# Dilated attention of a transformer block computed as a near band and four residue classes, merged by maxima and sums

## The chip, the cores and the metric

One NeuronCore of a Trainium2 chip runs the whole program; the other cores do nothing. The metric is the device time of one execution in microseconds, the median of three runs. The hardware profiler recorded one further execution, and every row below comes from it. The engines have the profile's names: PE is TensorE (PEld its weight loads), DVE is VectorE, ACT is ScalarE, POOL is GpSimd, SP is the engine whose queue issues nearly all DMAs.

## The reference

Two transformer layers for 1024 tokens of width 1024. The change lies in the first layer's attention, which has two kinds of heads, eight of each:

```
# dilated heads (depth 64): three patterns (window, dilation), each a softmax of its own
DILATED_PATTERNS = ((128, 1), (512, 4), (2048, 16))
for window, dilation in DILATED_PATTERNS:
    # each query attends to positions i + j*dilation, |j| <= window / (2*dilation)
    o, lse = dilated_window_attention(q, k, v, rel_bias, dilation, window // (2 * dilation))
w = softmax(stack(lses)); out_a = sum(w * outs)      # merged by softmax denominators
# latent heads (nope 64 + rope 32): dense softmax attention over all 1024 keys
out_b = mixer_mla(c_q, c_kv, k_rope, ...)
```

The bias of a dilated head depends only on the distance of key and query (32 buckets). With dilation 1 a query reaches keys at most 64 positions away; with dilations 4 and 16 it reaches only keys in its own residue class modulo 4. The rest of the layer (output projection, routed experts) and the second layer come after and are not touched.

## The kernel before, in words

The program is a row of stages, each with its own buffers, with a barrier between them. `front` projects the tokens and leaves q, k and v of all heads in DRAM, and for each dilated head a skewed table of bias plus the logarithm of the number of patterns that hold the distance (-1e30 where none does). So the three patterns become one dense masked softmax. Stage `att` then runs `attend_heads` over 16 heads, first the eight dilated ones, then the eight latent ones.

A head is cut into 8 units of 128 queries against all 1024 keys. Every engine has a program of its own, a loop over steps n, and works at unit n minus some lag:

- PE: `score(n)`, `turn_p(n-2)` (transposes of the probabilities), `weigh_half(n-4)` (probabilities times values, for two units at once, 256 columns wide), and for every second unit `turn_back`.
- DVE: the row maxima of unit n (for a dilated head one pass, L385, that also adds the table), then for unit n-2 the low halves `pT_lo` (L396) of the probabilities: float32 operands are split into a high and a low part for the matmuls.
- ACT: the high halves `pT_hi` (L343) of unit n-2, then the exponentials of unit n with their row sums.
- POOL: splits the next head's q, k and v into high and low parts.
- SP: for head j the loads of q, k, table and v, then the store of head j-2, in program order, each behind its semaphore waits.

Scores, probabilities and biased scores each have two buffers; the transposed probabilities in PSUM (`pT_ps`) and the weighed sum (`oT_ps`) have one. Engines work strictly in the order of their programs, and so does SP's queue.

## Time and profile before

| | us |
|---|---|
| median of 3 runs (4217.86 to 4221.16) | 4218.14 |
| the profiled execution | 4229.26 |
| its span | 4227.5 |
| attention stage, first to last row maximum | 275.6 to 679.9 |
| PE busy over the span | 3820.9 (90%) |
| DVE, ACT, POOL busy over the span | 2119.5, 1981.5, 1233.9 |

The span is the time from the first to the last instruction of the profiled execution; that execution took 1.8 us more than its span. The attention stage is about a tenth of the program. Busy time of PE counts matmuls whose ends overlap, so that a busy PE is not a PE at its peak.

### The profile page before, as it was taken

The numbers are of one execution on the slowest core, as the hardware profiler recorded it, in microseconds if no ns is written. First come the engines' busy times: TensorE is split into PE (matmuls) and PEld (weight loads), VectorE is DVE, ScalarE is ACT, GpSimd is POOL, SyncE is SP. The second block draws the span as 40 slices with busy tenths as digits, with TensorE's granted clock in tenths as the row PEclk, the third lists the DMA queues.
The fourth block names the chain that finished last, engine by engine and source line by source line (L and its number), as shares of the span: only waits on it lengthen the run. The fifth ranks groups of instructions, "written<-read, shape, count | busy, mean of one in ns | idle before, by whom it ended". The sixth has DMA issues, their size and how long they took to land. (4 is left out here: it accounts for less than half of the span.)

```text
span 4227.5 us, 55120 instructions
## 1 busy us (share of the span) xinstructions
PE 3820.9 (90%) x20567; PEld 3209.4 (76%) x20567; DVE 2119.5 (50%) x3777; ACT 1981.5 (47%) x3487; POOL 1233.9 (29%) x732
## 2 busy tenths in 40 slices
PE   8989997969986999999488875797999999999998
PEld 6879996847755777887388875797888768888886
DVE  3348875267754333320566757674234237533453
ACT  5248766337756545522366654564324234323331
POOL 0024430000004322311133244121631103876541
PEclk9999998969998999999699997998999999999999
DMA  3744223479957222222322212113653112222542
GB/s 118 251 134 118 51 51 105 184 273 420 421 241 255 90 80 80 89 94 74 90 61 79 80 55 79 46 46 115 227 161 117 68 50 90 87 88 85 188 148 98
DMA packets 336536, 548.38 MB, mean 130 GB/s; under 512 B 116451, under 2 KB 209507, under 8 KB 325219
## 3 DMA queue, kind: packets, MB, share of 16 engines
q1 hardware_dynamic: 318348, 478.76, 34.1%
q10 hardware_dynamic: 10720, 39.85, 2.4%
q0 software_dynamic: 7200, 26.22, 1.6%
q8 instruction: 166, 2.72, 0.3%
q14 instruction: 102, 0.84, 0.1%
HBM read 400.63 MB, written 144.11 MB: 129 GB/s over the span
## 5 line engine op out<-in xcount | busy, mean ns | idle before, releaser
L2739 POOL TENSOR_TENSOR mid_w_lo<-mid_w_raw,mid_w_hi 128x1024 fp32r<-128x1024 f32 (+1 forms) x64 | 153.0, 2395 | 406.2 <-ACT mid_w_hi L2927 406.2
L3473 POOL TENSOR_TENSOR end_w_lo<-end_w_raw,end_w_hi 128x1024 fp32r<-128x1024 f32 x60 | 147.2, 2460 | 334.4 <-ACT end_w_hi L3815 334.3
L3097 PE MATMUL mid_ps<-mid_w_hi,mid_xT_hi 128*128 128x512 f32 x576 | 229.0, 398 | 2.7 <-DVE mid_xT_lo L2801 2.7
L3097 PE MATMUL mid_ps<-mid_w_lo,mid_xT_hi 128*128 128x512 f32 x576 | 224.7, 390 | 0.0
L3097 PE MATMUL mid_ps<-mid_w_hi,mid_xT_lo 128*128 128x512 f32 x576 | 224.7, 390 | 0.0
L4131 PE MATMUL end_ps<-end_w_hi,end_xT_hi 128*128 128x512 f32 x544 | 214.7, 395 | 0.0
L4131 PE MATMUL end_ps<-end_w_hi,end_xT_lo 128*128 128x512 f32 x544 | 212.3, 390 | 0.0
L4131 PE MATMUL end_ps<-end_w_lo,end_xT_hi 128*128 128x512 f32 x544 | 211.9, 390 | 0.0
L957 DVE SCALAR_TENSOR_TENSOR moe_w_lo<-moe_wgu,moe_gcol,moe_w_hi 128x512 fp32r<-128x512 f32 x272 | 185.5, 746 | 7.7 <-ACT moe_w_hi L1097 7.7
L343 ACT ACTIVATE att_pT_hi<-att_pT_ps 128x512 fp32r<-128x512 f32 x256 | 139.1, 596 | 99.7 <-PE att_pT_ps L36 99.6
L1097 ACT ACTIVATE moe_w_hi<-moe_wgu,moe_gcol 128x512 fp32r<-128x512 f32 x272 | 173.2, 715 | 2.5 <-DMA moe_wgu<-in_w_gate_up 2.5
L3477 POOL TENSOR_TENSOR end_w_lo<-end_w_raw,end_w_hi 128x1024 fp32r<-128x1024 f32 x60 | 149.0, 2488 | 68.4 <-ACT end_w_hi L3829 68.4
L918 POOL DMA_INDIRECT moe_xb<-xrows,moe_idx x34 | 32.3, 951 | 467.1 <-PE moe_x_ps L36 272.9
L396 DVE TENSOR_TENSOR att_pT_lo<-att_pT_ps,att_pT_hi 128x512 fp32r<-128x512 f32 x256 | 163.6, 681 | 1.9 <-ACT att_pT_hi L343 1.9
L3097 PE MATMUL mid_ps<-mid_xT_hi,mid_w_hi 128*128 128x512 f32 (+1 forms) x400 | 155.9, 390 | 0.0
L3097 PE MATMUL mid_ps<-mid_xT_lo,mid_w_hi 128*128 128x512 f32 (+1 forms) x400 | 155.9, 390 | 0.0
L3097 PE MATMUL mid_ps<-mid_xT_hi,mid_w_lo 128*128 128x512 f32 (+1 forms) x400 | 155.9, 390 | 0.0
L2828 DVE SCALAR_TENSOR_TENSOR mid_conv<-mid_raw,mid_taps,mid_conv 128x1024 f32<-128x1024 f32 x96 | 145.6, 1517 | 3.4
L3503 POOL TENSOR_TENSOR end_w_lo<-end_w_raw,end_w_hi 128x1024 fp32r<-128x1024 f32 x44 | 110.2, 2511 | 122.4 <-ACT end_w_hi L3867 122.4
L4168 PE MATMUL end_ps<-end_w_hi,end_xT_hi 128*128 128x512 f32 x352 | 137.8, 391 | 2.9 <-issue 2.9
L286 PE MATMUL att_oT_ps<-att_pT_hi,att_v_both 128*128 128x256 f32 x512 | 137.8, 303 | 0.5 <-ACT att_oT L334 0.5
L4168 PE MATMUL end_ps<-end_w_hi,end_xT_lo 128*128 128x512 f32 x352 | 137.6, 391 | 0.0
(641 smaller groups left out, 11565.8 us busy)
## 6 DMA issues: line engine op xcount, KB each, us to landing
moe_wgu<-in_w_gate_up SPq DMA_DIRECT2D x34, 2048.0 KB, 11.6
moe_wd<-in_w_down SPq DMA_DIRECT2D x34, 1024.0 KB, 14.1
mid_w_raw<-in_w_in SPq DMA_DIRECT2D x60, 512.0 KB, 4.0
end_w_raw<-in_w_ffn_out SPq DMA_DIRECT2D x44, 512.0 KB, 3.7
end_w_raw<-in_w_ffn_in SPq DMA_DIRECT2D x40, 512.0 KB, 4.3
expert_rows<-moe_out ACTq DMA_DIRECT2D x34, 512.0 KB, 11.3
in_tail<-mid_y SPq DMA_DIRECT2D x56, 256.0 KB, 2.1
qkvT<-mid_conv SPq DMA_DIRECT2D x24, 512.0 KB, 4.4
```

What stands on the lines that cost most here:

```text
L286: ins = pe.matmul(oT_ps[:, 0:2 * P], v, part[:, m % 2, c], start=(c == 0 and k == 0), stop=(c == NT - 1 and k == len(parts) - 1))
L343: act.activation(pT_hi[:, m % 2, at, u * P:(u + 1) * P], pT_ps[:, at], ACT.Copy).then_inc(hi_p, 1)
L396: dve.tensor_tensor(pT_lo[:, m % 2, at, u * P:(u + 1) * P], pT_ps[:, at], pT_hi[:, m % 2, at, u * P:(u + 1) * P].bitcast(F32), ALU.subtrac ...
L957: dve.scalar_tensor_tensor(out=w_lo[:, n % 2, k], in0=wgu[:, n % GR, k], scalar=gcol[:, k:k + 1], in1=w_hi[:, n % 2, k].bitcast(F32), op0= ...
L1097: act.activation(w_hi[:, n % 2, k], wgu[:, n % GR, k], ACT.Copy, scale=gcol[:, k:k + 1]).then_inc(w_hi_set, 1)
L2739: pool.tensor_tensor(w_lo[:, c % 2, 2 * q:2 * q + 2, 0:wid], w_raw[:, 2 * q:2 * q + 2, 0:wid], w_hi[:, c % 2, 2 * q:2 * q + 2, 0:wid].bitc ...
L2828: ins = dve.scalar_tensor_tensor(out=conv[:, j], in0=src, scalar=w, in1=conv[:, j], op0=ALU.mult, op1=ALU.add)
L3097: ins = pe.matmul(o_, lhsT, rhs, start=(k == 0 and part == 0), stop=(k == KC - 1 and part == 2))
L3473: pool.tensor_tensor(halves(w_lo, piece), w_raw[:, 2 * q:2 * q + 2], halves(w_hi, piece).bitcast(F32), ALU.subtract).then_inc(w_split, 1)
L3477: pool.tensor_tensor(slot_of(w_lo, s), factor[s % 7], slot_of(w_hi, s).bitcast(F32), ALU.subtract).then_inc(w_split, 1)
L4131: ins = pe.matmul(o_, lhsT, rhs, start=(k == 0 and part == 0), stop=(k == KC - 1 and part == 2))
L4168: ins = pe.matmul(ps[:, 2 * t + j], xx[:, i % 8, t * P:(t + 1) * P], down_slot(ww, i)[:, j], start=(k == 0 and part == 0), stop=(k == KB - ...
```

## The change

`front` now takes the tokens in residue order (all tokens that are 0 modulo 4, then 1, 2, 3), so q, k and v of all heads lie in that order in DRAM, and the outputs are stored back in natural order. The bias row of a head shrinks from 2048 to 1184 numbers.

A new function `attend_both` replaces `attend_heads` for the first layer (the second layer still calls `attend_heads`). Its heads alternate: dilated, latent, dilated, latent. A latent head is computed as before, in 8 units. A dilated ("sparse") head has 4 units. Unit t holds four segments of 128 queries by 256 keys: two of the near band (32 positions of each of the four residue classes as queries, 64 of each class as keys) and two of the far part (128 queries of class t against the 256 keys of the class). Each segment has its own maximum, exponential and sum. The weighed sum of a segment is no longer transposed: the probabilities are the stationary operand, the values (high and low half side by side, 128 columns) the moving one, and DVE adds the two halves (`tensor_reduce` into `keep`). The near results are in another query order than the far ones, so SP writes them to a DRAM tensor `near` (four DMAs) and reads them back (one); then DVE takes the higher maximum (`highest`), ACT the weights, DVE the shares, and POOL makes the merged output.

```
+            @block.sync
+                def load_table(j):
...
+                    first, second, far = jobs[j]["bias"]
+                    for w in range(2):
+                        sp.dma_start(view[:, w + 1, 0], first).then_inc(table_in[i % 2], 16)
+                        sp.dma_start(view[:, w, 1], second).then_inc(table_in[i % 2], 16)
+                    sp.dma_start(view[:, 0, 0, :, EDGE:], first[:, :, EDGE:]).then_inc(table_in[i % 2], 16)
+                    sp.dma_start(view[:, 2, 1, :, 0:EDGE], second[:, :, 0:EDGE]).then_inc(table_in[i % 2], 16)
+                    for c in range(STRIDE):
+                        sp.dma_start(table[c * BLOCK:(c + 1) * BLOCK, i % 2, 3 * SEG:], far[c]).then_inc(table_in[i % 2], 16)
...
+                def move_near(j):
+                    i = rank[j]
+                    sp.wait_ge(kept, sparse_by[last_unit[j]])
+                    for c in range(STRIDE):
+                        dst = jobs[j]["near"][c * CLASS:(c + 1) * CLASS].rearrange("(t u) d -> u t d", u=BLOCK)
+                        sp.dma_start(dst, keep[c * BLOCK:(c + 1) * BLOCK, i % 2, 0]).then_inc(near_out, 16)
+                    sp.wait_ge(near_out, 16 * STRIDE * (i + 1))
+                    sp.dma_start(keep[:, i % 2, 2], jobs[j]["near"].rearrange("(t p) d -> p t d", p=P)).then_inc(near_in, 16)
...
+                for i in range(H // 2 + 1):
+                    if i < H // 2:
+                        load(2 * i)
+                        load(2 * i + 1)
+                    if i:
+                        move_near(2 * i - 2)
+                        store(2 * i - 2)
+                        store(2 * i - 1)
...
+                def weigh_sparse(n):
...
+                    outcome_taken(n)
+                    pe.wait_ge(lo_p, 2 * n + 2)
+                    for g in range(SEGS):
+                        i = 2 * t + g % 2
+                        for b in range(2):
+                            v = near_both[:, rank[j] % 2, i + b] if g < 2 else v_both[:, j % 2, 2 * t + b]
+                            for k, part in enumerate((pT_hi, pT_lo)):
+                                ins = pe.matmul(oT_ps[:, g * P:(g + 1) * P], split_at(part, n)[:, 2 * g + b], v,
+                                                start=(b == 0 and k == 0), stop=(b == 1 and k == 1))
...
+                def tops_sparse(n):
...
+                    for g in range(SEGS):
...
+                        ch.add(dve.tensor_tensor_reduce(biased[:, n % 2, here], s_ps[:, n % 2, here], table[:, i, at:at + SEG],
+                                                        1.0, -3e38, ALU.add, ALU.max, keep[:, i, g // 2, w, DV:DV + 1]))
+                    ch.wait()
...
+                def highest(j):
+                    both = keep[:, rank[j] % 2, 1:3]
+                    dve.wait_ge(near_in, 16 * (rank[j] + 1))
...
+                for n in range(U + 6):
+                    for j in range(0, H, 2):
+                        if n == last_unit[j] + 7:
+                            highest(j)
+                    if n >= 5 and n - 5 < U and is_sparse[n - 5]:
...
+                        dve.tensor_reduce(keep[:, rank[j] % 2, 0:2, 2 * t:2 * t + 2, 0:DV], found, AX.X, ALU.add).then_inc(kept, 1)
...
+                        if not sparse[j] and n == last_unit[j] + 6:
...
+                            dve.tensor_tensor(o[:, j % 2], o_ps[:], inverse[:, i % 2].unsqueeze(2).to_broadcast([P, NT, DV]), ALU.mult).then_inc(o_out, 1)
...
+                def merge(j):
+                    i = rank[j]
+                    pool.wait_ge(share_set, i + 1)
...
+                for j in range(H):
+                    if j:
+                        split_queries(j)
+                    if sparse[j]:
+                        order_queries(j)
+                    if j:
+                        split_keys(j)
+                    split_values(j)
...
+                    if sparse[j] and j:
+                        merge(j - 2)
...
-    attend_heads(nc, "att", ident, dilated + latent)
+    attend_both(nc, "att", ident, dilated, latent)
```

**SP's queue, around one dilated head.** Before, in the middle of the dilated heads: the store of a head (L223, which waits for that head's `o_out`), then the loads two heads ahead (names are the tiles, "<-" their source).

```order
L223 DMA mixed<-att_o 128x8x64 [waits att_o_out]
L197 DMA att_qT<-qkT_a 64x1024 [waits att_split_q]
L199 DMA att_qT<-qkT_a 64x1024
L206 DMA att_kT<-qkT_a 64x1024 [waits att_split_k]
L208 DMA att_kT<-qkT_a 64x1024
L213 DMA att_table<-skew 128x1920 [waits att_topped]
L219 DMA att_v<-v_a 128x8x64 [waits att_split_v]
```

After, the end of one turn of SP's loop: ahead of these rows stand the four stores of the latent head before (L630, waits `att_o_out`), four loads of q and k and ten of the table.

```order
L591 DMA att_v<-v_a 128x8x64 [waits att_split_v]
L596 DMA att_v_near<-v_a 16x64
L597 DMA att_v_near<-v_a 32x8x64
L602 DMA att_v_near<-v_a 32x9x64 x2
L599 DMA att_v_near<-v_a 32x8x64
L600 DMA att_v_near<-v_a 16x64
L557 DMA att_qT<-qkT_b 96x1024 [waits att_split_q]
L565 DMA att_kT<-qkT_b 96x1024 [waits att_split_k]
L591 DMA att_v<-v_b 128x8x64 [waits att_split_v]
L619 DMA near<-att_keep 32x8x66 [waits att_kept]
L619 DMA near<-att_keep 32x8x66 x3
L621 DMA att_keep<-near 128x8x66 [waits att_near_out]
```

The copy of the near results out and back (L619, L621) stands in the queue behind four stores and all loads for the next two heads, 28 DMAs in all.

**DVE, the row maxima of one unit of a dilated head.** Before: one pass over 1024 columns with its read of the maximum, then the low halves of unit n-2.

```order
L383 MEMSET att_pad 128x1 [waits att_exped,att_scored]
L385 ISA att_biased,att_top<-att_s,att_table 128x1024
L385 ISA att_top 128x1
L389 TENSOR_SCALAR att_neg_top<-att_top 128x1 [waits att_dve_steps]
L396 TENSOR_TENSOR att_pT_lo<-att_pT_ps,att_pT_hi 128x4x128 [waits att_hi_p] x2
```

After: four passes over 256 columns, each with its read.

```order
L819 MEMSET att_pad 128x1 [waits att_exped,att_scored]
L827 ISA att_biased,att_keep<-att_s,att_table 128x256
L827 ISA att_keep 128x1
L827 ISA att_biased,att_keep<-att_s,att_table 128x256
L827 ISA att_keep 128x1
L827 ISA att_biased,att_keep<-att_s,att_table 128x256
L827 ISA att_keep 128x1
L827 ISA att_biased,att_keep<-att_s,att_table 128x256
L827 ISA att_keep 128x1
L830 TENSOR_SCALAR att_neg_top<-att_keep 128x4 [waits att_dve_steps]
L871 TENSOR_TENSOR att_pT_lo<-att_pT_ps,att_pT_hi 128x512 [waits att_hi_p] x2
```

The unit has the same 1024 columns of scores but there are half as many units; the passes are four.

**DVE, inside the latent head that follows a dilated one.** After, the end of its fifth step, all of its sixth, and its seventh up to the first low halves; before, such a step has only a maximum, its scaling and two low halves.

```order
L871 TENSOR_TENSOR att_pT_lo<-att_pT_ps,att_pT_hi 128x4x128 [waits att_hi_p] x2
L859 TENSOR_REDUCE att_top<-att_s 128x1 [waits att_exped,att_scored]
L860 TENSOR_SCALAR att_neg_top<-att_top 128x1 [waits att_dve_steps]
L871 TENSOR_TENSOR att_pT_lo<-att_pT_ps,att_pT_hi 128x4x128 [waits att_hi_p] x2
L836 TENSOR_TENSOR att_higher<-att_keep 128x8 [waits att_near_in]
L837 TENSOR_TENSOR att_gap<-att_keep,att_higher 128x16 [waits att_dve_steps]
L859 TENSOR_REDUCE att_top<-att_s 128x1 [waits att_exped,att_scored]
L860 TENSOR_SCALAR att_neg_top<-att_top 128x1 [waits att_dve_steps]
L871 TENSOR_TENSOR att_pT_lo<-att_pT_ps,att_pT_hi 128x4x128 [waits att_hi_p] x2
```

The wait for the near results (`att_near_in`) stands ahead of the seventh step's row maximum and low halves.

## Rows read from the trace of the kernel before

**Rows 1.** The score tile's readers: ns min/median/max, first and last start

```profile
L385 DVE CUSTOM_DVE_ANT_0 att_biased<-att_s,att_table x64: 1219/1220/1225, 275.6 to 459.6; 128x1024 f32<-128x1024 f32 x64
L388 DVE TENSOR_REDUCE att_top<-att_s x64: 1211/1225/1226, 462.8 to 679.9; 128x1 f32<-128x1024 f32 x64
```

**Rows 2.** Windows: us; busy PE, PEld, DVE, ACT, POOL; PEclk, DMA share, GB/s

```profile
300.00:460.00 160.00, 160.00 (x1184) 147.97 (x1183) 143.34 (x339) 129.47 (x242) 69.63 (x39) 1.00 0.36 92
470.00:680.00 210.00, 210.00 (x1466) 190.90 (x1465) 162.41 (x261) 143.89 (x274) 68.05 (x39) 1.00 0.19 41
```

**Rows 3.** Timeline of TensorE over one latent unit: start us, us, instruction

```profile
560.85 0.55 PE L302 MATMUL att_o_ps<-att_fold,att_oT 128*128 128x64 f32 x4
561.21 0.47 PE L261 MATMUL att_s<-att_k_hi,att_q_hi 96*128 96x512 f32 x1
...
562.67 1.04 PE L36 MATMUL att_pT_ps<-att_ident,att_p 128*128 128x128 f32 x8
563.47 0.37 PE L286 MATMUL att_oT_ps<-att_pT_hi,att_v_both 128*128 128x256 f32 x1
...
564.50 0.40 PE L261 MATMUL att_s<-att_k_hi,att_q_hi 96*128 96x512 f32 x1
```

**Rows 4.** Timeline of VectorE over one dilated unit

```profile
370.27 1.22 DVE L385 CUSTOM_DVE_ANT_0 att_biased<-att_s,att_table 128x1024 f32<-128x1024 f32 x1 [0.59 <-issue]
...
371.42 0.08 DVE L385 DVE_READ_ACCUMULATOR2_ANT att_top<- 128x1 f32 x1
371.54 0.15 DVE L389 TENSOR_SCALAR att_neg_top<-att_top 128x1 f32<-128x1 f32 x1
371.61 1.28 DVE L396 TENSOR_TENSOR att_pT_lo<-att_pT_ps,att_pT_hi 128x512 fp32r<-128x512 f32 x2
```

**Rows 5.** A 256-wide tile of the last stage, the same view as rows 1

```profile
L3612 DVE TENSOR_REDUCE end_soft<-end_ps x32: 414/424/426, 3366.9 to 3431.5; 128x1 f32<-128x256 f32 x32
...
L3941 ACT ACTIVATE end_scratch<-end_ps,end_soft x32: 468/473/478, 3367.5 to 3436.3; 128x256 f32<-128x256 f32 x32
```

**Rows 6.** 128-column matmuls of the delta stage, timeline and tile view

```profile
2145.54 1.05 PE L1940 MATMUL delta_ps<-delta_inv,delta_Z 128*128 128x128 f32 x8
...
L1940 PE MATMUL delta_ps<-delta_inv,delta_Z x512: 272/276/582, 2094.9 to 2554.7; 128*128 128x128 f32 x171
```

**Rows 7.** Timeline of SP's queue, attention stage and delta stage

```profile
386.06 0.59 SPq L197 DMA_DIRECT2D att_qT<-qkT_a  x1
386.69 0.60 SPq L199 DMA_DIRECT2D att_qT<-qkT_a  x1
...
2049.02 3.77 SPq L1427 DMA_DIRECT2D delta_lower<-delta_L  x8
2054.04 0.49 SPq L1432 DMA_DIRECT2D delta_small<-delta_lower  x1
```

**Rows 8.** DMA issues of three stretches: xcount, KB each, median us to landing

```profile
mixed<-att_o SPq DMA_DIRECT2D x7, 256.0 KB, 2.7
...
att_qT<-qkT_a SPq DMA_DIRECT2D x16, 256.0 KB, 4.4
...
att_v<-v_b SPq DMA_DIRECT2D x6, 256.0 KB, 5.7
...
delta_lower<-delta_L SPq DMA_DIRECT2D x64, 16.0 KB, 1.7
```

**Rows 9.** Query splitting on POOL in the attention stage, tile view

```profile
L418 POOL TENSOR_TENSOR att_q_hi<-att_qT,att_one x9: 1890/1893/1905, 277.5 to 462.0; 128x1024 fp32r<-128x1024 f32 x7, 96x1024 fp32r<-96x1024 f32 x2
L421 POOL TENSOR_TENSOR att_q_hi<-att_qT,att_q_hi x7: 2388/2395/2414, 279.5 to 416.9; 64x1024 fp32r<-64x1024 f32 x7
```

**Rows 10.** Timeline of POOL at the start of the attention stage

```profile
266.71 0.10 POOL L445 MEMSET att_one<- 128x1 f32 x1 [265.82 <-issue]
```

**Rows 11.** Windows around an idle stretch of TensorE, columns as in rows 2

```profile
1230.00:1236.20 6.20, 0.34 (x4) 0.11 (x1) 1.47 (x3) 2.43 (x5) 0.00 (x0) 0.85 0.21 85
1236.20:1241.20 5.00, 4.90 (x16) 4.26 (x17) 5.00 (x8) 5.00 (x8) 0.00 (x0) 0.50 0.00 0
```

More of the change, by code:

```diff
@@ L21 @@
 SLOTS = 4
+STRIDE = 4
+NEAR, AFAR = 96, 512
+BIAS = (2 * STRIDE - 1) * NEAR + AFAR
+NEVER = -1e30
 @contextmanager
@@ new lines, in bias_constants, with reach @@
+def bias_constants(T, buckets, max_distance, patterns):
+    block, edge = P // STRIDE, P // STRIDE // 2
+    steps = np.arange(NEAR)[None] - (block + edge - 1)
+    near = (STRIDE * steps + np.arange(1 - STRIDE, STRIDE)[:, None]).reshape(-1)
+    far = STRIDE * (np.arange(AFAR) - (T // STRIDE - 1))
+    def reach(rel, pairs):
+        n = np.abs(rel)
+        return sum(((n % d == 0) & (n // d <= w // (2 * d)) & (n < T)).astype(np.float64) for w, d in pairs)
+    assert all(d == 1 or d % STRIDE == 0 for w, d in patterns)
+    rel = np.concatenate([near, far])
+    count = np.concatenate([reach(near, [(w, d) for w, d in patterns if d == 1]), reach(far, [(w, d) for w, d in patterns if d > 1])])
@@ L2523, in _ @@
                 pe.wait_ge(hot_in, 32)
-                for b in range(4):
-                    pe.matmul(ps[0:A_HEADS, 4 + b], values[:], onehot[:, b * BANK:(b + 1) * BANK], start=True, stop=True).then_inc(hot_done, 1)
+                for b in range(BIAS_BANKS):
+                    wid = min(BANK, BIAS - b * BANK)
+                    pe.matmul(ps[0:A_HEADS, 4 + b, 0:wid], values[:], onehot[:, b * BANK:b * BANK + wid], start=True, stop=True).then_inc(hot_done, 1)
                 pe.wait_ge(const_in, 16)
@@ L4210, in table @@
-    def table(h):
-        return skew[h:h + 1, P - 1:P - 1 + P * W - P].rearrange("h (p w) -> (h p) w", w=W - 1)[:, 0:W - P]
-    dilated = [dict(depth=A_DIM, dv=A_DIM, q=qkT_a[h * A_DIM:(h + 1) * A_DIM], k=qkT_a[AW + h * A_DIM:AW + (h + 1) * A_DIM],
-                    v=tiles(v_a[:, h * A_DIM:(h + 1) * A_DIM]), out=tiles(mixed[:, h * A_DIM:(h + 1) * A_DIM]),
-                    scale=A_DIM ** -0.5, bias=table(h)) for h in range(A_HEADS)]
-    latent = [dict(depth=NOPE + ROPE, dv=B_DIM, q=qkT_b[h], k=qkT_b[B_HEADS + h],
-                   v=tiles(v_b[:, h * B_DIM:(h + 1) * B_DIM]),
-                   out=tiles(mixed[:, AW + h * B_DIM:AW + (h + 1) * B_DIM]), scale=(NOPE + ROPE) ** -0.5, bias=None) for h in range(B_HEADS)]
@@ L4219, in build_program, with tables, block, far @@
-    attend_heads(nc, "att", ident, dilated + latent)
+    mixed, near = dram("mixed", (T, AW + B_HEADS * B_DIM)), dram("near", (A_HEADS, T, A_DIM + 2))
+    def tables(h):
+        rows, width, pitch = P // STRIDE, BIAS - 1, STRIDE * NEAR
+        def block(ahead):
+            at = (STRIDE - 1) * NEAR + rows - 1 + ahead
+            flat = skew[h, at:at + P * width].rearrange("(p w) -> p w", w=width)
+            return flat[:, 0:pitch].rearrange("p (c z) -> p c z", z=NEAR)[:, :, 0:rows]
+        def far(c):
+            at = c * (rows * width + NEAR - rows) + (2 * STRIDE - 1) * NEAR + P - 1
+            return skew[h, at:at + rows * width].rearrange("(p w) -> p w", w=width)[:, 0:3 * P]
+        return block(0), block(rows), [far(c) for c in range(STRIDE)]
@@ new lines, in by_class_out @@
+    def by_class_out(columns):
+        return mixed[:, columns].rearrange("(h p c) d -> c p h d", c=STRIDE, p=P)
+    dilated = [dict(depth=A_DIM, dv=A_DIM, q=qkT_a[h * A_DIM:(h + 1) * A_DIM], k=qkT_a[AW + h * A_DIM:AW + (h + 1) * A_DIM],
+                    v=v_a[:, h * A_DIM:(h + 1) * A_DIM], out=by_class_out(slice(h * A_DIM, (h + 1) * A_DIM)),
+                    scale=A_DIM ** -0.5, bias=tables(h), near=near[h]) for h in range(A_HEADS)]
+    latent = [dict(depth=NOPE + ROPE, dv=B_DIM, q=qkT_b[h], k=qkT_b[B_HEADS + h], v=v_b[:, h * B_DIM:(h + 1) * B_DIM],
+                   out=by_class_out(slice(AW + h * B_DIM, AW + (h + 1) * B_DIM)), scale=(NOPE + ROPE) ** -0.5, bias=None) for h in range(B_HEADS)]
```

456 lines of the change are left out of this document (435 added, 21 removed).

## The prediction

> **What bounds the kernel now.** Only the attention stage changes much, so I read that stage alone. First the view of the score tile gives its pace: the row maxima of the 64 dilated units start from 275.6 to 459.6 us, those of the 64 latent units from 462.8 to 679.9 [rows 1]. Divided by 63 that is 2.92 us per dilated unit and 3.45 per latent unit; 64 of each make 407.7 us. Then the windows show which engine fills it: PE is busy all of 160.00 and 210.00 us at full clock; DVE is busy 143.34 and 162.41 of it, ACT 129.47 and 143.89 [rows 2]. PE sets the pace of both kinds. In a latent unit DVE works 162.41/210 x 3.45 = 2.67 us, so it has 0.8 to spare; the dilated part has all engines close together.
>
> The timeline splits PE's latent unit [rows 3]: scores from 561.21 to 562.67 (1.46 us), transposes to 563.47 (0.80), weighing to 564.50 (1.03), and every second unit 0.36 of turning back (560.85 to 561.21): 3.47 with half of the last, as measured.
>
> **A sparse unit.** Eight score matmuls of 256 columns: the eight weighing matmuls of 256 columns took 1.03 [rows 3], so 1.0. Transposes 0.80 as before. In the four steps of a sparse head PE still weighs latent units (1.03 + 0.18), because weighing lags by four steps; so these steps cost PE 3.0.
>
> DVE: before, the pass over 1024 columns took 1.15 until its read, 0.12 to the scaling, 0.07 to the low halves, 1.28 for both [rows 4]. A reduction over 256 columns takes 0.424 where one over 1024 takes 1.225 [rows 1, 5], so a pass over 256 saves 0.80: 0.35 until its read, and 0.11 for the read. Four are 1.85 and the step is 1.85 + 0.07 + 1.28 + some 0.15 of waits = 3.35. The low bound is PE's 3.0; the high one 4.1, if no pass starts before the last has fully ended (4 x (0.42 + 0.12 + 0.12) = 2.65 in place of 1.85). I take 3.35, since the trace shows DVE's ends overlapped. ACT was busy 129.47/160 x 2.92 = 2.36 per unit; four exponentials at 0.473 [rows 5] in place of one of 1024 columns (1.22, if ACT's takes as long as DVE's) add 0.7, so 3.1, below DVE.
>
> **The latent steps behind it.** In the first four latent steps PE weighs sparse units: 16 matmuls of 128 columns. The delta stage issues eight such in 1.05 us, of which 0.276 is the last one's own time [rows 6]: 0.110 apart, so 16 take 1.78 with 0.1 to begin. The step is 3.45 - 1.03 - 0.18 + 1.88 = 4.12. DVE's new sum of halves is a 512-wide pass like one low half, 0.64 [rows 4]; with 2.67 it is 3.3 and lies under PE.
>
> The Trainium skill ("TensorE: Matmul & The Clock Gate", section "Back-to-back issue gap") gives 81 ns for a sustained 128-column matmul with its weight load. By that 16 would be 0.5 us cheaper and the 32 such steps 16 us, and the kernel would come to about 4211 us. The row shows 0.110, in a run of eight like the sixteen here, and the sum goes by the row; the rule gets no chance of its own.
>
> A pair (4 sparse, 8 latent units) is then 4 x 3.35 + 4 x 4.12 + 4 x 3.45 = 43.7. The merge's small operations on DVE add some 0.5 where its slack is used up. POOL adds 0.3: after the shares it merges (estimate 1.9 + 1.3) and splits the next latent head's q and k, 1.9 + 2.4 each [rows 9], 11.8 in all, while the sparse head lasts 13.4 and the score must be there 1.6 earlier. So 44.5 a pair, 356 for eight, **51.7 us less** than 407.7.
>
> **Start and end.** POOL starts its program at 266.71 [rows 10] and now clears pads first, on which the first table load waits; the first score also waits for the reordered queries, one POOL pass of 1.9 [rows 9]: 2 us. Before the first latent head POOL splits two sets of values (passes of 512 and 576 columns, about half of those of 1024, 4.6 us after they land) and then q and k (8.6) [rows 9]: 13.2 against a sparse block of 13.4, with the landing of some 4 us ahead of it: 4 us. Three more stores at the end, 0.47 each: 1.3. Together **7.3 us more**. The front's shorter bias moves fewer bytes with more DMAs under a PE that is busy: nothing; uncovered it would be 24 DMAs of 0.47, 11 us.
>
> **The wait that I expect.** Let latent head B follow sparse head A. DVE waits for A's near results at B's seventh step, ahead of that step's maximum and low halves; behind it wait ACT's exponential, PE's transposes and so everything. The near copy stands in SP's queue behind 28 DMAs, and the first of these, a store of the latent head before A, waits for an output that DVE makes at the end of B's second step. From there:
> - Issue: 4 stores and 17 table and value loads at 3.77/8 = 0.47, six q and k loads at 386.69 - 386.06 = 0.63, one more value load: 14.1 us [rows 7].
> - Near out: 1.4 to the start of the fourth issue; the landing of such a write 1.7 [rows 8]. In the delta stage SP in fact waits for eight small writes, from 2049.02 + 3.77 to 2054.04, before it reads them back [rows 7].
> - Near in: 1024 pieces of 264 bytes; a store of the same size and 256-byte pieces lands in 2.7 [rows 8]; I take 3.0. Sum 20.3.
> - Queue: a value load right behind a latent head's q and k takes 5.7 [rows 8], 2.7 more. Between 0 and 2.7 I take 2.7, since the copy stands just there. Sum 23.0.
>
> DVE needs it after steps three to six, 2 x 4.12 + 2 x 3.45 = 15.1, and 0.8 of slack: 15.9. It is **7.1 us late** (bounds 0, if the issues overlap more than in rows 7, and 14, if each of the 28 takes the longest spacing, 0.63, and the queue counts for the way out and the way in). PE falls idle, and after an idle stretch the trace shows it at half clock: 6.2 us idle, then 5.0 at a granted clock of 0.50 [rows 11], the lower of the two levels (1.2 GHz). That costs up to 2.5, here 1.7. So 8.8 a pair, in six pairs of eight: the first pair's copy and the last one's have no loads ahead of them that wait. **53 us more.**
>
> Sum: -51.7 + 7.3 + 53 = +9. The profiled execution of 4229.3 would take 4238. The median of the runs lies 11 us lower; I add the same 9 to 4218: **4227 us**.
>
> **Rivals.**
> - *The copy is in time.* If the 28 issues and the round trip take under 16 us, nothing waits and 51.7 - 7.3 = 44 us are won: 4174. For it: the eight writes of the delta stage were issued at 0.47 and had all landed 1.25 us after the last issue [rows 7], without a backlog. Against it: even without a queue the sum is 20.3. It decides at 15.9 us from the latent output. With halfway cases, 0.25.
> - *The sparse unit is DVE's.* At the high bound of 4.1, 0.75 x 4 x 8 = 24 us more: 4251. For it: four short passes and four reads that depend on one semaphore. Against it: DVE's passes overlap in rows 4. 0.15.
> - *Small pieces choke the DMA queue.* Table, near values and near results now move in pieces of 64 to 264 bytes, before the table moved in 7680. If each 256 KB of these took 1 us longer, some 5 us a pair would fall on the copy, 30 us in six pairs: 4257. Against it: 256 KB in 256-byte pieces lands in 2.7 us, in pieces of 4 KB in 4.4 [rows 8]. The Trainium skill ("DMA: Bandwidth & Descriptors", section "Specifications") asks for at least 512 bytes a transfer for line rate; rows 8 show no such loss. 0.15.
> - *No change that can be told.* A measurement of this kernel can tell about 0.2%, 8.4 us. My forecast lies just outside this band and half of its cases inside it.
>
> **How the numbers follow.** The forecast (copy late by 4 to 9 us, 4210 to 4250) has 0.45. Faster: the first rival's 0.25 and 0.05 of the forecast, 0.30. Within 0.2%: 0.22, nearly all of it the forecast's. Slower: the rest of the forecast 0.18, and the two slow rivals 0.30: 0.48. The range reaches from the copy in time to the far end of the slow rivals, 4178 to 4275; beyond lie the page's cheap matmuls on top of the first rival, and two slow rivals at once.
>
> **What would show it.** Right: sparse steps of 3.3 us with DVE full, four latent steps of 4.1 with PE full; DVE idle 5 to 8 us ahead of `att_higher` (L836) once a pair from the second on, released by a DMA from `near`, and PE at 0.5 behind it; SP issuing without a pause for some 14 us ahead of L619. Wrong: no such idle time, then the time falls by 40 us; or sparse steps near 4 us; or the landing of `near` far longer than 3 us.

## The result and the profile after the change

| | before | after |
|---|---|---|
| median of 4 runs, us | 4219.65 (4217.86 to 4223.98) | 4261.58 (4258.21 to 4266.70) |
| the profiled execution | 4229.26 | 4266.70 |
| its span | 4227.5 | 4264.6 |
| first to last instruction of the attention stage | 429.2 | 467.9 |

The kernel before has one run more here than above. The ratio is 1.0099 (95% interval 1.0081 to 1.0116): the change costs 42 us in the medians and 37 in the profiled executions. The forecast was 4227, +9, in a range of 4178 to 4275: the direction and the range hold, the size does not.

The stage tells where. The tile view of `near`, the DRAM copy of the near results (SP's two lines that move it, and who waits for it):

```profile
L619 SPq DMA_DIRECT2D near<-att_keep x32: 303/472/1576, 310.8 to 702.1; - x32
L621 SPq DMA_DIRECT2D att_keep<-near x8: 376/377/380, 314.9 to 704.3; - x8
...
  DVE att_higher L836: 73.6, 7
DMA to landing us min/median/max: 1.8/4.7/5.7
```

VectorE is idle for 73.6 us in seven waits for the copy: 1.0 in the first pair of heads, 72.6 in the next six, 12.1 each (11.5 to 12.7). The eighth does not wait. VectorE's timeline at the second pair:

```profile
360.56 0.15 DVE L860 TENSOR_SCALAR att_neg_top<-att_top 128x1 f32<-128x1 f32 x1
360.63 1.28 DVE L871 TENSOR_TENSOR att_pT_lo<-att_pT_ps,att_pT_hi 128x512 fp32r<-128x512 f32 x2
374.25 0.17 DVE L836 TENSOR_TENSOR att_higher<-att_keep 128x8 f32<-128x8 f32 x1 [12.34 <-DMA att_keep<-near]
374.46 0.18 DVE L837 TENSOR_TENSOR att_gap<-att_keep,att_higher 128x16 f32<-128x16 f32 x1
374.56 1.21 DVE L859 TENSOR_REDUCE att_top<-att_s 128x1 f32<-128x1024 f32 x1
```

TensorE stops with it. In the windows around that wait and over two whole pairs (columns as in [rows 2]) it is idle from 366.2 to 376.7, works at the granted clock 0.50, the lower level (1.2 GHz), up to about 382, and a pair lasts 58 us of which it is busy for 46:

```profile
366.00:376.00 10.00, 0.16 (x1) 0.00 (x0) 1.68 (x5) 0.01 (x1) 3.63 (x3) 0.64 0.50 93
376.00:379.00 3.00, 2.30 (x11) 2.33 (x12) 2.96 (x5) 2.22 (x5) 0.00 (x0) 0.50 0.00 0
379.00:382.00 3.00, 3.00 (x16) 3.00 (x15) 1.47 (x6) 1.75 (x4) 1.19 (x1) 0.50 0.00 0
...
383.60:441.68 58.08, 46.12 (x322) 42.16 (x322) 39.29 (x93) 31.22 (x78) 29.19 (x18) 0.88 0.36 74
441.68:499.48 57.80, 46.11 (x321) 42.13 (x320) 39.33 (x92) 31.08 (x78) 29.19 (x18) 0.88 0.37 74
```

Why the copy is late stands in SP's timeline of the same pair. `o_out`, the semaphore on which the store of the latent head before waits, was set at 347.33, and SP issued without a pause from there to the copy:

```profile
328.40 20.86 SPq L630 DMA_DIRECT2D mixed<-att_o  x8
349.30 0.48 SPq L557 DMA_DIRECT2D att_qT<-qkT_a  x1
...
354.02 1.75 SPq L580 DMA_DIRECT2D att_table<-skew  x1
...
356.36 2.29 SPq L583 DMA_DIRECT2D att_table<-skew  x4
...
363.17 0.43 SPq L591 DMA_DIRECT2D att_v<-v_b  x1
363.64 3.08 SPq L619 DMA_DIRECT2D near<-att_keep  x4
371.33 0.38 SPq L621 DMA_DIRECT2D att_keep<-near  x1
```

(The first row holds eight stores, the last four of them from 347.35 to 349.26.) The near sums had been complete at 355.32; their copy was issued 8.3 us later because of its place in the queue (experiment 1 shows that nothing else held it).

The other lines answer to [rows 3] and [rows 4] and show the work itself as it was worked out. One of the latent steps that weigh a sparse unit, on TensorE: 16 weighing matmuls of 128 columns (first two and last), then the next score.

```profile
351.82 1.04 PE L40 MATMUL att_pT_ps<-att_ident,att_p 128*128 128x128 f32 x8
352.61 0.30 PE L710 MATMUL att_oT_ps<-att_near_both,att_pT_hi 128*128 128x128 f32 x1
352.75 0.28 PE L710 MATMUL att_oT_ps<-att_near_both,att_pT_lo 128*128 128x128 f32 x1
...
354.32 0.28 PE L710 MATMUL att_oT_ps<-att_v_both,att_pT_lo 128*128 128x128 f32 x1
354.43 0.45 PE L676 MATMUL att_s<-att_k_hi,att_q_hi 96*128 96x512 f32 x1
```

They take 354.43 - 352.61 = 1.82 us, 0.112 apart behind the first; 1.88 was forecast, and the step lasts 4.06 in place of 4.12. The 81 ns of the Trainium skill ("TensorE: Matmul & The Clock Gate", section "Back-to-back issue gap") do not appear here either.

One line has no counterpart in the forecast: VectorE's scaling of four maxima (L830, 128x4). Its view, and one of its long ones behind the passes of its step (the first two and the last read), with POOL's instruction that ran beside it:

```profile
L830 DVE TENSOR_SCALAR att_neg_top<-att_keep x32: 169/524/1741, 274.2 to 682.6; 128x4 f32<-128x4 f32 x32
...
389.89 0.41 DVE L827 CUSTOM_DVE_ANT_0 att_biased<-att_s,att_table 128x256 f32<-128x256 f32 x1
390.24 0.08 DVE L827 DVE_READ_ACCUMULATOR2_ANT att_keep<- 128x1 f32 x1
390.24 0.41 DVE L827 CUSTOM_DVE_ANT_0 att_biased<-att_s,att_table 128x256 f32<-128x256 f32 x1
...
390.93 0.08 DVE L827 DVE_READ_ACCUMULATOR2_ANT att_keep<- 128x1 f32 x1
391.04 1.73 DVE L830 TENSOR_SCALAR att_neg_top<-att_keep 128x4 f32<-128x4 f32 x1
392.68 1.27 DVE L871 TENSOR_TENSOR att_pT_lo<-att_pT_ps,att_pT_hi 128x512 fp32r<-128x512 f32 x2
...
390.33 2.40 POOL L919 TENSOR_TENSOR att_k_lo<-att_kT,att_k_hi 96x1024 fp32r<-96x1024 f32 x1
```

It lasts 0.17 us where POOL is idle and 1.73 here; it ends at 392.77, POOL's instruction at 392.73. Below such an instruction is called held. 22 of the 32 scalings are long, and each ends 0.02 to 0.03 us behind a POOL instruction. In the kernel before none of the 128 scalings (128x1) lasts over 0.16.

### The profile page after: what moved, and what is told of

Same layout as the page of the kernel before. It is cut to its first block and busy times, and to the rows that moved or that the text cites. A ratio compares the mean times of both kernels' runs of the same rounds, so it can differ in the third digit from the quotient of the medians.

```text
span 4264.6 us, 54593 instructions
## 1 busy us (share of the span) xinstructions
PE 3773.8 (88%) x20181; PEld 3166.8 (74%) x20181; DVE 2087.5 (49%) x3841; ACT 1925.4 (45%) x3526; POOL 1296.6 (30%) x782
## 5 line engine op out<-in xcount | busy, mean ns | idle before, releaser
L4666 PE MATMUL end_ps<-end_w_hi,end_xT_lo 128*128 128x512 f32 x544 | 212.0, 390 | 0.0
L4666 PE MATMUL end_ps<-end_w_lo,end_xT_hi 128*128 128x512 f32 x544 | 211.7, 389 | 0.0
L40 PE MATMUL att_pT_ps<-att_ident,att_p 128*128 128x128 f32 x768 | 111.5, 289 | 69.5 <-DVE att_pT_lo L871 64.4
L40 PEld LDWEIGHTS att_pT_ps<-att_ident,att_p 128*128 128x128 f32 x768 | 94.7, 149 | 86.3 <-issue 67.8
L784 ACT ACTIVATE att_pT_hi<-att_pT_ps 128x512 fp32r<-128x512 f32 x192 | 104.5, 592 | 106.5 <-PE att_pT_ps L40 106.5
L4703 PE MATMUL end_ps<-end_w_lo,end_xT_hi 128*128 128x512 f32 x352 | 138.0, 392 | 0.0
```

The source lines that it names most:

```text
L40: return pe.transpose(out, tile, ident[:])
L4666: ins = pe.matmul(o_, lhsT, rhs, start=(k == 0 and part == 0), stop=(k == KC - 1 and part == 2))
L4703: ins = pe.matmul(ps[:, 2 * t + j], xx[:, i % 8, t * P:(t + 1) * P], down_slot(ww, i)[:, j], start=(k == 0 and part == 0), stop=(k == KB - ...
```

## Experiments

Each number of the kernel before stands beside runs on the same chip; the ratio of the changed kernel, to compare with, is 1.0099. "A pair" is the time from the first maxima of one sparse head to those of the next, read from VectorE's timeline; "a sparse step" goes from the start of one scaling of the maxima to the next, so that the first begins in the last latent step. Profiles are compared by the length of the attention stage, since the stages behind it, with the same code in all 14, differ by up to 12 us among them.

**1. The latent head's store later in SP's order**

```diff
+                    if i >= 2:
+                        store(2 * i - 3)
                     if i:
                         move_near(2 * i - 2)
                         store(2 * i - 2)
-                        store(2 * i - 1)
+                store(H - 1)
```

Expected: 

> The edit moves only the latent head's four stores in SP's order: behind the loads for the next two heads and ahead of the near copy one turn later, so the loads no longer stand behind a store that waits for `o_out`. Theory A (the near copy is late because of its place in SP's queue): in six pairs the wait at `att_higher` falls from 12.1 us (11.5 to 12.7) to under 1.5, a pair lasts about 45 us as the undisturbed last one does (44.9) in place of 57.8, and the kernel gains 6 x 12.9 = 77 us: 4262 - 77 = 4185, range 4175 to 4200. Theory B (the loads' own traffic holds the copy, wherever it stands): the copy still takes over 10 us from the last kept sum to its landing and the wait stays at 5 us or more: over 4215. Theory C (the wait hides another one, such as POOL's splitting of the next head): the wait goes, but a pair stays above 50 us: over 4215 too, with the idle time at another instruction.

Measured: 4187.05 us beside 4225.61, ratio 0.9913 (0.9897 to 0.9930). The view of the waiting line, L838 in this kernel:

```profile
L838 DVE TENSOR_TENSOR att_higher<-att_keep x8: 173/173/175, 318.1 to 628.3; 128x8 f32<-128x8 f32 x8
...
  DMA att_keep<-near: 3.6, 6
```

The wait fell from 73.6 us to 3.6, and a pair lasts 44.5 us: six in a row lie between 44.50 and 44.55. The first write is issued 0.03 us after the last kept sum, and from the second pair on the results are back 6.7 to 7.3 us after it. Theory A holds; this change of order alone was worth 1.0099 - 0.9913 = 0.0186, 79 us.

**2. The near copy on ScalarE's queue**

```diff
+                        if n == last_unit[j] + 5:
+                            near_away(j)
+                        if n == last_unit[j] + 6:
+                            near_back(j)
```

`near_away` waits for the kept sums and issues the four writes, `near_back` waits for them and issues the read.

Expected: 

> The near copy, out and back, is issued by ScalarE's queue instead of SP's; SP keeps its order for the rest. Theory A (place in SP's queue): the four writes leave within 3 us of the last kept sum, the results land back some 7 us after it, the wait at `att_higher` falls from 12.1 to 0 to 3 us, and 60 to 75 us are won, less at most 8 for ScalarE's five issues a pair at 0.5: 4190 to 4210. Theory B (the traffic of SP's loads on the DMA engines holds the copy): the writes go out at once but take 5 us to land and the read more than 3; the wait stays at 5 or more: over 4220.

Measured: 4234.11 us, ratio 1.0022 (1.0011 to 1.0032). The tile view of `near`:

```profile
L753 ACTq DMA_DIRECT2D near<-att_keep x32: 309/482/724, 315.5 to 669.4; - x32
L758 ACTq DMA_DIRECT2D att_keep<-near x8: 382/383/442, 319.5 to 671.9; - x8
...
  DVE att_higher L844: 46.4, 8
  ACT att_p L808: 7.4, 4
DMA to landing us min/median/max: 1.8/3.1/7.8
```

The writes left 1.6 us after the last kept sum, as theory A has it, but the results came back late all the same: waits of 4.8 to 8.0 us in the six pairs. At the second pair the read took 7.8 us to land (2.9 in the changed kernel), while SP issued its loads beside it, from the table at 355.32 to the latent values at 366.87. In the first and the last pair, where no loads were under way, the read on the same queue took 3.0. By its time and its waits this is theory B: a queue of its own ends the wait to be issued, 5.0 of the 12.1 us, and not the delay beside the loads. The core's DMA engines were busy for 0.98 of the time while the second pair's read was under way, 0.45 and 0.41 in the first and the last pair; that the loads' packets kept it waiting there is likely, not tested by itself. The first experiment ends both, since it moves the loads ahead: there, from the second pair on, the last write lands in 2.2 to 2.6 us and the read in 2.9 to 3.4.

**3. The table in longer pieces** (one execution)

```diff
-                        sp.dma_start(view[:, w + 1, 0], first).then_inc(table_in[i % 2], 16)
+                        sp.dma_start(table[:, i % 2, (w + 1) * SEG:(w + 1) * SEG + P], wide[:, 0:P]).then_inc(table_in[i % 2], 16)
```

and so for all six near loads of the table, which then holds other numbers than the biases. Expected: 

> The six near loads of a head's table fetch rows of 128 neighbouring numbers, pieces of 512 bytes (768 of them) in place of 3072 pieces of 128 and 64; the count of DMAs stays, the values are not the table's. Theory A (the 28 issues and the queue behind the latent head's q, k and v make the copy late): the wait at `att_higher` falls by 2 us at most, the stall of 1.2 us in issuing the fifth table load: 4250 to 4262. Theory B (small pieces choke the queue): the wait falls by 5 us or more, 30 us in six pairs: under 4235.

Measured: 4254.02 us. The waits are 64.8 us in seven, 10.6 in each of the six pairs in place of 12.1; the first write goes out 15.0 us after `o_out` in place of 16.7, mostly since the fifth table load (1.75 us above) now takes 0.43, and the writes still take 5.4 to land. Theory A: the table's small pieces cost 1.5 us of the 12. The fifth load:

```profile
357.01 0.43 SPq L579 DMA_DIRECT2D att_table<-skew  x1
```

**4. Ten issues fewer** (one execution)

```diff
-                    if sparse[j]:
+                    if sparse[j] and rank[j] < 2:
                         load_table(j)
...
```

The later heads use the tables of the first two, and VectorE waits for these alone. Expected: 

> The table loads of the third to eighth sparse head are left out (these heads use the tables of the first two, so the values are wrong); everything else is as in the changed kernel. Of the 28 issues ahead of the near copy 10 go. Theory A (the issues' number is the larger part of the lateness): the first write of the copy is issued 5.5 to 6.5 us earlier after `o_out` (16.7 before), lands as late as before (5 us, behind the latent head's q, k and v), and the wait at `att_higher` falls from 12.1 to 5.5 to 7: 30 to 40 us in six pairs, 4225 to 4237. Theory B (the table's small pieces choke the queue): the landing of the writes falls from 5 us to 2.5 too, and the wait to 4 or less: under 4220.

Measured: 4237.66 us. The first write goes out 10.7 us after `o_out`, 6.0 earlier; the writes still take 5.7 to land; the waits are 6.2 to 6.9 us in the six pairs, 6.5 on average. Theory A, 0.7 us beyond its far end in time: ten issues of 28 are 5.6 of the 12.1 us.

**5. Four scalings of one column**

```diff
-                    dve.tensor_scalar(neg_top[:, n % 4].rearrange("p (k s) -> p k s", k=2), keep[:, i, 0:2, 2 * t:2 * t + 2, DV],
-                                      -jobs[j]["scale"], None, ALU.mult).then_inc(topped, 1)
+                    for g in range(SEGS):
+                        w = 2 * t + g % 2
+                        ins = dve.tensor_scalar(neg_top[:, n % 4, g:g + 1], keep[:, i, g // 2, w, DV:DV + 1],
+                                                -jobs[j]["scale"], None, ALU.mult)
+                    ins.then_inc(topped, 1)
```

Expected: 

> The edit replaces VectorE's one scaling of four maxima (128x4) by four scalings of one column (128x1); the order of all queues stays. In the changed kernel the 128x4 scaling lasts 0.17 us when POOL is idle and up to 1.74 when POOL is in a tensor_tensor, and 22 of 32 end 0.02 to 0.03 us after the POOL instruction that ran. Theory A (VectorE is held by the running POOL instruction, which a one-column scaling is not, as in the latent units, where none is held): the 3.1 us a pair of held time go, the sparse steps of 3.5, 3.95 and 4.3 us come to 3.0 to 3.3, minus some 0.2 for three more scalings: 2 to 2.5 us a pair, 16 to 20 in all, 4242 to 4246. Theory B (the long records are only drawn to the next instruction, and something else sets the step): no change within 5 us, 4262, and the four scalings' rows show the same time in another place.

Measured: 4250.79 us, ratio 1.0064 (1.0048 to 1.0081): by the ratios 15 us under the changed kernel, by the medians and by the stage (456.7 us) 11, less than the 16 to 20 expected. The view of the line, which answers to that of L830:

```profile
L832 DVE TENSOR_SCALAR att_neg_top<-att_keep x128: 142/145/155, 273.4 to 672.5; 128x1 f32<-128x1 f32 x128
```

No scaling is held, though POOL runs beside them as before, and the third sparse step lasts 2.95 us in place of 3.9 to 4.1 (five of the pairs). That VectorE was held is theory A; a pair won 1.0 us by it (six pairs), not 2 to 2.5, and the first pair 3.3.

**6. Later store and four scalings**

Expected: 

> The later store of the first experiment (0.9913 of the kernel before, 44.5 us a pair) together with the four one-column scalings of the second. In the run with the scalings alone the one pair whose copy was not late lasted as long as with the one wide scaling (17.12 us from the last latent maximum to the next latent one, 17.22 with the later store), though VectorE's 1.7 us hold was gone. Theory A (then POOL is the bound: it splits the latent head's q and k right behind the merge, and the first latent score waits for it): no gain over the first experiment, 44.2 to 44.5 a pair, within 3 us of its time, and TensorE's first latent score waits for POOL. Theory B (VectorE's hold sets the sparse block): 1.3 us or more a pair, 10 us less in all.

Measured: 4174.05 us, ratio 0.9881 (0.9864 to 0.9897). A pair lasts 43.95 us, and the stage 380.7 in place of 389.6 of the first experiment: seven pairs give 0.57 each and the first pair 5, where the second and third latent steps no longer run at the half clock (4.4 and 4.1 us in place of 7.7 and 5.5). That is neither theory: more than A's nothing, less a pair than B's 1.3, though the sum comes near B's 10. The windows of one pair of the first experiment and of two of this one:

```profile
359.20:403.70 44.50, 43.54 (x323) 39.56 (x321) 38.34 (x93) 30.99 (x78) 29.18 (x17) 1.00 0.47 97
...
364.94:408.88 43.94, 43.08 (x322) 39.61 (x321) 36.95 (x104) 31.13 (x77) 29.18 (x18) 1.00 0.48 98
408.88:452.83 43.95, 43.10 (x322) 39.62 (x321) 36.86 (x105) 31.20 (x77) 29.19 (x18) 1.00 0.49 98
```

TensorE is busy for 43.1 of 43.95 us, but with the hold it was 43.5 of 44.5, the same 98%: its busy share does not tell which engine is the bound. In the first experiment VectorE works without a pause through the first 13.4 us of a pair, nearly the whole sparse head; here it does so through three steps (9.0 us) and then waits 0.9 us. From the first scaling's start to the low halves the four steps took 2.54 us with the hold and take 1.04 here; of these 1.5 us a pair only 0.57 show. That TensorE sets the rest is likely and not shown.

**7. POOL's merge behind the next latent head's split**

```diff
+                    if not sparse[j] and j >= 2:
+                        merge(j - 3)
                     split_values(j)
...
-                    if sparse[j] and j:
-                        merge(j - 2)
```

Expected, with the one wide scaling: 

> The later store, and POOL's merge of a sparse head moved behind the splitting of the next latent head's q and k; the one wide scaling stays. Theory A (POOL's chain merge, then split, sets when the first latent score can start, and its instructions hold the wide scaling): POOL starts to split some 4 us earlier, but its instructions still run beside the scalings, so that VectorE is held as before by up to 1.7 us a time: a pair of 43.5 to 44.5, 0 to 8 us less than the first experiment. Theory B (POOL alone is the bound): 2 us a pair, 16 in all. Theory C (the later merge delays store, loads and with them the copy): slower than the first experiment by over 5 us, with a wait at `att_higher`.

Expected, with the four scalings: 

> All three: later store, four one-column scalings, later merge. Theory A (VectorE held by POOL and POOL's chain are two bounds of one length, so that only both together move it): sparse steps of 2.95 to 3.1 throughout, a sparse block shorter by some 2 us, a pair of 42.3 to 43, 12 to 17 us less than the first experiment: a ratio of 0.987 to 0.989 to the kernel before. Theory B (TensorE or ScalarE already sets the sparse steps): within 4 us of the first experiment.

Measured: ratios 0.9998 (0.9989 to 1.0008) and 0.9993 (0.9983 to 1.0002): 36 and 47 us slower than the same kernels without this edit. All theories of both fell. There is no wait for the copy to speak of (1.0 us at most); the first sparse step lasts 8.9 us in place of 3.7. VectorE's timeline there and POOL's, in the kernel with the wide scaling:

```profile
369.38 1.97 DVE L878 TENSOR_TENSOR att_scaled<-att_keep,att_weight 128x16 f32<-128x16 f32 x1
371.38 1.81 DVE L879 TENSOR_TENSOR att_summed<-att_scaled 128x8 f32<-128x8 f32 x1
373.22 0.20 DVE L880 RECIPROCAL att_merged_inv<-att_summed 128x8 f32<-128x8 f32 x1
373.46 2.15 DVE L883 TENSOR_TENSOR att_share<-att_weight,att_merged_inv 128x16 f32<-128x16 f32 x1
...
368.93 2.38 POOL L906 TENSOR_TENSOR att_q_lo<-att_qT,att_q_hi 96x1024 fp32r<-96x1024 f32 x1
371.28 1.89 POOL L919 TENSOR_TENSOR att_k_hi<-att_kT,att_one 96x1024 fp32r<-96x1024 f32 x1
373.25 2.33 POOL L921 TENSOR_TENSOR att_k_lo<-att_kT,att_k_hi 96x1024 fp32r<-96x1024 f32 x1
```

The three small operations with two operands in SBUF, 0.17 us each when POOL is idle, end 0.02 to 0.03 us behind the POOL instruction that was running (371.31, 373.17, 375.58); the reciprocal between them, with one operand, is not held. The first sparse step's 5.2 us more in seven pairs are 36.7 us, where the stage lost 36.3 and, with the four scalings, 43.4. They are not all of a pair's loss, which is 5.9 and 6.3 us: behind the idle time TensorE works at the granted clock 0.50, and a step that took 2.95 us takes up to 5.0. In the kernel with the four scalings (columns as in [rows 2]):

```profile
379.00:382.00 3.00, 2.58 (x12) 2.61 (x13) 2.96 (x16) 2.88 (x11) 1.27 (x1) 0.50 0.19 42
382.00:384.50 2.50, 2.50 (x14) 2.50 (x13) 0.82 (x2) 2.23 (x9) 0.00 (x0) 0.50 0.62 140
```

With the wide scaling the first pair gave some 4 us back: its latent steps ran at the full clock from 292 us on, in the first experiment not before 299.

**8. The start**

With experiment 7's second kernel the first latent head's q and k were also loaded ahead of the table and split ahead of the first values, q even ahead of the sparse head's reordered queries. Expected: 

> As the one before, and at the start of the stage the first latent head's q and k are loaded ahead of the table and split by POOL ahead of the first values. In the changed kernel POOL splits them from 278.7 to 287.3 us, the first latent score waits for it, and the steps behind it last 7.7 and 5.5 us at the half clock. Theory A: the first latent maximum comes 5 to 8 us earlier after the first sparse one (16 to 19 us before), so 5 to 8 us less than the one before. Theory B (the first sparse unit now waits for its table, or POOL's values come late for the first weighing): under 2 us gained.

Measured: ratio 0.9975 (0.9965 to 0.9984). The first latent maximum comes 10.4 us after the first sparse one in place of 19.2, the first sparse one 3.9 later, and the stage takes 418.7 us in place of 424.2. Theory A, though the first sparse maximum took back nearly half.

**9. The split waits for the shares**

Added to experiment 7's second kernel. Where the early start comes with it, q is split behind the reordered queries.

```diff
                 for j in range(H):
+                    if not sparse[j] and j >= 2:
+                        pool.wait_ge(share_set, rank[j])
                     if j:
                         split_queries(j)
```

Expected: 

> Later store, four one-column scalings, and POOL's merge behind the split of the next latent head's q and k as in the two slow kernels, but the split now waits for the shares first, so that none of POOL's instructions runs beside VectorE's three small operations with two operands in SBUF (scaled, summed, share), which lasted 1.8 to 2.2 us each there, in place of 0.17. Theory A (those three held operations were the whole loss of the later merge): the first sparse step comes back from 8.9 to 3.7 us, the first latent score no longer waits for the merge's 3.2 us, a pair lasts 42.9 to 43.9 us (43.95 with the later store and the scalings alone), and the ratio to the kernel before is 0.985 to 0.988. Theory B (the later merge delays something else, such as the store and with it the loads): a pair stays above 45 us and the ratio above 0.992.

Expected, with the early start: 

> As the one before, and at the start of the stage the first latent head's q and k are loaded ahead of the table and split ahead of the first values, behind the reordered queries. Theory A: the first latent maximum comes 10 to 11 us after the first sparse one (19 without it, 10.4 in the slow kernel that had this start), the first sparse one no more than 2 us later: 5 to 7 us less than the one before. Theory B (the table or the values come late instead): under 2 us less.

Measured: 0.9933 (0.9916 to 0.9949) and, with the start, 0.9911 (0.9894 to 0.9927). The three operations are at 0.17 us again and the first sparse step at 3.7 to 5.3, so that much of theory A holds; but the copy waits again, 1.3 to 4.9 us in six pairs (3.1 to 4.5 with the start), a pair lasts 45.5 to 48.6 us in five of the six, and both the pair and the ratio are theory B's. The sparse head's own store now waits for the later merge, and the loads stand behind it; experiment 10 tests this. The start gives another 8.6 us of the stage, more than the 5 to 7 expected.

**10. Both stores later**

Against experiment 9's kernel with the early start:

```diff
...
                     if i >= 2:
                         store(2 * i - 3)
+                        store(2 * i - 4)
                     if i:
                         move_near(2 * i - 2)
-                        store(2 * i - 2)
+                store(H - 2)
                 store(H - 1)
```

Expected: 

> As the one before, with the sparse head's four stores moved behind the next loads too, ahead of the near copy one turn later. In the two runs before, the sparse block fell to 16.6 us from the last latent maximum to the next latent one (17.1 with the later store and the scalings alone), but the copy was late again by 2.8 to 4.9 us: the sparse head's store waits for the later merge and the loads stand behind it. Theory A (that store is the only reason): the wait at `att_higher` falls under 1 us in all pairs, a pair lasts 43.3 to 43.6 us (43.95 there), the start gives another 5 us: a ratio of 0.985 to 0.987 to the kernel before, the fastest of all. Theory B (the loads are held by something else, such as the split they overwrite): the wait stays above 2.5 us and the ratio above 0.989.

Measured: 4167.08 us beside 4226.28, ratio 0.9861 (0.9844 to 0.9877), the fastest here and 59 us under the kernel before. The waits are 4.7 us in six, at most 1.1, so the store was what held the loads. A pair lasts 43.88, not the 43.3 to 43.6 expected:

```profile
402.87:446.75 43.88, 43.08 (x322) 39.57 (x321) 36.96 (x104) 31.05 (x77) 29.17 (x18) 1.00 0.45 94
```

TensorE's 43.08 is that of experiment 6, and the later merge gave 0.07 us a pair; what this kernel has over experiment 6, 8.4 us of the stage, is the start. The intervals of the two ratios overlap; the stage's lengths, 372.3 and 380.7, are one execution each.

## Why the prediction was right in direction and short in size

The mechanism, the direction and the range held; the term that was mis-sized is the late copy. The forecast's own band, a copy late by 4 to 9 us and 4210 to 4250, missed. The bounds of its lateness (0 to 14 us) held the 12.1; but the range's upper end was set by two slow rivals that both fell, so that 4262 lies inside is in part luck. The sum, term by term; the stage's measured difference is 467.9 - 429.2 = 38.7 us.

| term | forecast | measured | from |
|---|---|---|---|
| eight pairs without the wait | -51.7 | -51.7 | 44.5 a pair in experiment 1 |
| start and end of the stage | +7.3 | +12 | the rest of the stage's 38.7 |
| late copy, six pairs | +53 | +79 | 57.6 a pair less 44.5, times 6 |
| front | 0 | -5.4 | start of the attention stage, 262.6 and 257.2 |

- *The pairs.* 43.7 + 0.5 + 0.3 came out to the tenth by chance, since two errors cancel: four sparse steps took 14.2 us in experiment 1 (3.69, 3.02, 3.22, 4.30), not 4 x 3.35 = 13.4, and the latent ones less. VectorE's four passes start 0.344 apart, 1.5 us with the last read, not the 1.85 that was taken, since a pass starts with the read of the one before; the held scaling of L830, 2.2 us a pair more than four unheld ones of 128x4, put the time back. The rival of a 4.1 us sparse step fell with the overlap of its passes; single steps of 4.3 us there are, but not by its cause.
- *The late copy* is the mechanism that was forecast, at the instruction, in the pairs and with the releaser that were named: experiment 1 removes it by order alone. Its size was wrong. Of the chain from `o_out`, the issues took 16.7 us on average over the six pairs, not 14.1; the start of the fourth write 2.0, not 1.4; the writes 5.1 to land, not 1.7 + 2.7; the read 2.9, near the 3.0 taken: 26.7 in place of 23.0. VectorE needed the results 14.6 us after `o_out`, not 15.9: the four steps take 2 x 4.06 + 2 x 3.23, since the two latent ones hold none of the turning back that is in the mean of 3.45, and the slack of 0.8 was not there. So it was late by 12.1, not 7.1. Of the 5.0 us the issue term is the largest part, 2.6: a spacing taken from other stages left out the stall of the fifth table load (1.2 us, removed in experiment 3). At the half clock a pair lost 13.1 - 12.1 = 1.0 more, not 1.7.
- *The copy in time* was a rival at 4174. Experiment 1 makes it true: 0.9913 of 4219.65 is 4183.
- *Small pieces* as a bound of their own fell: the table's cost 1.5 us a pair (experiment 3), by SP's issue and not by the landing, and the near results, still in pieces of 264 bytes, land in 2.2 to 2.6 us out and 2.9 to 3.4 back once the loads are out of the way (experiment 1; 1.7 and 3.0 were forecast without a queue). The near values' pieces were not tested by themselves.
- *The queue term* was right in size and too narrow in kind. Experiment 2 shows that the loads delay a copy on another queue as well.
- *Start.* The first sparse maximum came 2.5 us later after the stage's start than before, the first pair lasted 52.4 us, 7.9 more than the later ones, and the end took 1.5 more. The forecast named POOL's splits at the start (4 us); it left out that TensorE, idle meanwhile, then ran two latent steps at the half clock (7.7 and 5.4 us, granted clock 0.50 from 287 to 300). Three stores of 0.47 are 1.4, not 1.3.
- *Front.* "Nothing" was wrong: the first matmuls of the program, which make the bias rows, are six and take 4.1 us in place of eight and 7.0, and they stand at the head of the program, where nothing covers them (before, then after):

```profile
7.08 6.99 PE L2525 MATMUL front_ps<-front_w_raw,front_values 33*8 33x512 f32 x8 [7.08 <-DMA front_values<-in_rel_bias]
...
6.12 4.11 PE L3060 MATMUL front_ps<-front_w_raw,front_values 33*8 33x512 f32 x6 [6.12 <-DMA front_values<-in_rel_bias]
```

  They end at 10.2 us in place of 14.1, 3.8 us earlier. The rest of the 5.4 is within the scatter: in all 13 executions with this front the stage starts at 255.8 to 261.1 us, 258.6 on average, 4.0 earlier than in the one before.

The stages behind attention have the same code in all 14 profiled executions, and their length runs from 3526 to 3538 us; the 4.8 us that they are longer after than before lie inside that.

## What to carry to other kernels

When a round trip through memory is added to an in-order DMA queue, find the slowest semaphore that anything ahead of it in the queue waits for, count from there every issue and every byte up to the trip's landing, and compare with the first instruction that needs it. Put work that waits for something late (a store) behind work that waits for nothing, before thinking of another queue. And when a new stall has a size, undo it by order alone first: the gain that was hidden behind it (here 44.5 us a pair, then 43.9) shows how much is left for the next bound.

## What the runs showed of the hardware beyond the forecast

- A VectorE tensor_scalar of 128x4 numbers in SBUF waits for the end of a POOL tensor_tensor that is running (0.17 us without one, up to 1.74); the same of 128x1 does not (0.142 to 0.155, all 128). A VectorE tensor_tensor with both operands in SBUF waits too (0.17, up to 2.2), one with an operand in PSUM does not: the low halves keep their 1.28 us a pair of passes beside POOL. The Trainium skill states this lock ("SBUF — State Buffer", section "Who interferes with whom"): VectorE shares one pair of SBUF ports with GpSimd and takes it in its two-port modes or for two SBUF inputs. The traces agree with the waiting, though no row shows a port, and they show how it reads in a profile: not as idle time ahead of the instruction, but as a long instruction that ends with POOL's.
- A DMA issued on ScalarE's queue into the middle of SP's loads (experiment 2, a read of 264 KB) took 4.6 to 7.8 us to land; with no loads beside it, it took 3.0.
- SP's issue of a load in 64-byte pieces behind four in 128-byte pieces took 1.6 to 2.2 us in the six pairs, of the same load in 512-byte pieces (experiment 3) 0.43.
